# One more quarter-tile of tokens by gathered expert rows, dense expert sums with columns on the partitions, and one-hot gate rows made four at a time with the gates applied on ScalarE

## What is computed

```python
def peer(h, w_query, sub_keys, u_emb, v_emb):
    q = (t @ w_query).reshape(T, PEER_HEADS, 2, PEER_HALF)
    s = jnp.einsum('thpk,pnk->thpn', q, sub_keys)
    s_val, s_idx = lax.top_k(s, PEER_TOPK)                      # 16 of 128, twice a head
    cand = s_val[..., 0, :, None] + s_val[..., 1, None, :]
    best, pos = lax.top_k(cand.reshape(T, PEER_HEADS, 256), PEER_TOPK)
    expert = ...                                                # 128 expert numbers a token
    gate = jax.nn.softmax(best, -1)
    act = jax.nn.gelu(jnp.einsum('td,ted->te', tb, u_emb[eb]), approximate=False) * gb
    return jnp.einsum('te,ted->td', act, v_emb[eb])
x = x + ga2 * peer(modulate(rmsnorm(x, g_ffn), sh2, sc2), ...)
return rmsnorm(x, g_final)
```

## Time and profile before

| | us |
|---|---|
| median of 3 runs | 3695.62 |
| lowest, highest | 3694.08, 3696.91 |
| the profiled execution, its time | 3693.22 |
| its span, first to last instruction | 3691.2 |
| PE busy in the span | 3508.3 |
| DVE busy | 2088.9 |
| POOL busy | 1987.5 |
| ACT busy | 1104.4 |

### The profile page before, as it was taken

The page is one execution under the profiler, slowest core; times in us unless marked ns, Lnnn a source line. Parts: engine busy times, 40 slices in busy tenths (PEclk is TensorE's granted clock), DMA queues, the critical chain, the costliest instruction groups (busy, mean ns, idle before and its releaser), DMA issues.

```text
span 3691.2 us, 46132 instructions
## 1 busy us (share of the span) xinstructions
PE 3508.3 (95%) x17646; PEld 3001.0 (81%) x17646; DVE 2088.9 (57%) x3619; ACT 1104.4 (30%) x1240; POOL 1987.5 (54%) x942
## 2 busy tenths in 40 slices
PE   5799999998889799999999999999999999999996
PEld 2477778874578589999999999999888888888885
DVE  1317561102521365995477777772566776667669
ACT  3221211123322223232344333443232232232222
POOL 0244432211333545677655565556677777777773
PEclk8799999999999899999999999999999999999998
DMA  9545552228632323777666777668898888888883
GB/s 344 208 162 181 186 179 75 79 71 296 249 125 93 124 90 134 250 295 276 250 259 262 292 283 282 258 261 342 319 338 315 311 311 309 317 321 313 305 308 111
DMA packets 291479, 874.83 MB, mean 237 GB/s; under 512 B 17361, under 2 KB 78081, under 8 KB 237216
## 3 DMA queue, kind: packets, MB, share of 16 engines
q1 hardware_dynamic: 226224, 519.08, 40.0%
q0 software_dynamic: 38704, 281.20, 18.7%
q10 hardware_dynamic: 26432, 73.02, 5.2%
HBM read 803.82 MB, written 69.37 MB: 237 GB/s over the span
## 4 chain that ended last, share of the span: by engine, by line
PE 83%; DVE 6%; DMA 5%; ACT 2%; POOL 2%; issue 1%; ACTq 1%; SPq 0%; DVEq 0%
PE bank L1753 76%; PE bank L2032 2%; PE bank L1946 2%; DMA neurons<-tiny 2%; PE bank L1761 2%; DMA ring<-in_w_mod 2%; DMA ring<-in_w_in 1%; PE bank L1925 1%; POOL ring_lo L432 1%; DVE low L1343 1%; DVE acc L1642 1%; ACT w_hi L425 0%; PE bank L2015 0%; DVE b L1531 0%; ACTq L734 0%
## 5 line engine op out<-in xcount | busy, mean ns | idle before, releaser
L692 POOL TENSOR_TENSOR split<-ring,split 128x1024 fp32r<-128x1024 f32 x544 | 1305.6, 2412 | 689.7 <-ACT split L1012 688.8
L1753 PE MATMUL bank<-h_hi,split 128*128 128x384 f32 (+1 forms) x4608 | 1221.0, 342 | 5.2 <-POOL split L692 3.7
L1753 PE MATMUL bank<-split,a_split 128*128 128x512 f32 x4608 | 1052.1, 390 | 17.1 <-DVE acc L1635 8.8
L1012 ACT ACTIVATE split<-ring 128x1024 fp32r<-128x1024 f32 x544 | 577.2, 1062 | 1595.0 <-PE bank L1753 1566.0
L1753 PEld LDWEIGHTS bank<-split,a_split 128*128 128x128 f32 x4608 | 867.4, 188 | 201.7 <-DVE acc L1635 6.2
L1753 PEld LDWEIGHTS bank<-h_hi,split 128*128 128x128 f32 x4608 | 838.0, 188 | 26.3 <-POOL split L692 4.6
L1753 PE MATMUL bank<-h_lo,split 128*128 128x384 f32 (+1 forms) x2304 | 784.0, 340 | 0.0
L432 POOL TENSOR_TENSOR ring_lo<-ring,w_hi 128x2048 fp32r<-128x2048 f32 x47 | 230.4, 4903 | 432.4 <-ACT w_hi L425 427.6
L1753 PEld LDWEIGHTS bank<-h_lo,split 128*128 128x128 f32 x2304 | 433.0, 188 | 9.9
L1635 DVE TENSOR_TENSOR acc<-acc,bank 128x512 f32<-128x512 f32 x360 | 244.4, 682 | 299.8 <-PE bank L1753 281.2
L1753 PE MATMUL bank<-hT_hi,w_hi 128*128 128x512 f32 (+1 forms) x768 | 292.0, 380 | 23.3 <-POOL ring_lo L432 18.5
(11 more groups left out here) (266 smaller groups left out, 3606.2 us busy)
## 6 DMA issues: line engine op xcount, KB each, us to landing
ring<-in_u_emb SPq DMA_DIRECT2D x128, 1024.0 KB
ring<-in_v_emb SPq DMA_DIRECT2D x128, 1024.0 KB
ring<-in_w_mod SPq DMA_DIRECT2D x96, 1024.0 KB
ring<-in_w_in SPq DMA_DIRECT2D x48, 1024.0 KB
neurons<-tiny ACTq DMA_DIRECT2D x128, 192.0 KB
gate_table<-b ACTq DMA_DIRECT2D x6, 4096.0 KB, 14.7
weigh<-neurons SPq DMA_DIRECT2D x32, 768.0 KB
weigh<-gate_table SPq DMA_DIRECT2D x32, 768.0 KB
```

What stands on the lines that cost most here:

```text
L692: nc.gpsimd.tensor_tensor(split[:, r % 2, 1, at].bitcast(F32R), ring[:, r % 4, :, :].rearrange("p k n -> p (k n)")[:, at], split[:, r % 2, ...
L1012: nc.scalar.activation(split[:, q % 2, 0, at].bitcast(F32R), ring[:, q, :, :].rearrange("p k n -> p (k n)")[:, at], ACT.Copy)\
L1753: last = mm(out_, left[a].bitcast(F32R), right[b].bitcast(F32R), start=start and n == 0, stop=stop and n == 2)
```

## The change

It does five things.

1. **Tokens.** The dense tokens become 352 (`TD = 352`, eleven pieces of 32). The 32 tokens 352 to 383 are computed by gathered rows too. They have 128 slots each, and since a gather brings 128 rows, four of a token's slots go into one gather: 32 more gathers in each stage, 160 instead of 128 (`SROWS`). ACT's DMAs spread their row numbers, gates and inputs over the partitions in unit 40 (12 small DMAs). Their dots (n from 128) take both inputs from SBUF (`h2_x` and the rows), and their sums go to `x_acc` in SBUF (both inputs of L1749 in SBUF). The gathers are placed by a formula: one a unit up to gather 34, then 125 in 88 units of the neuron stage (the new ones at units 102 to 124), and 159 in 119 units of the sum stage (the new ones at units 97 to 121).
2. **Neuron units.** The moving operand has 352 columns in place of 384, read as pieces of 32 tokens.
3. **Sum units.** Stationary is now a 128-column piece of `v_emb`'s split, moving is `a_split` with 352 tokens: 4 x 4 x 3 = 48 matmuls of 352 a unit in place of 36 of 512, and four banks of 352 columns a unit are flushed into `acc` [column, token]. At the end PE turns `acc` back, a quarter of the columns at a time (`turn_quarter`), and adds the four parts of the 32 tokens with one matmul.
4. **Gate groups.** 88 in place of 96. DVE makes the first-key rows of four tokens in one instruction, and the second-key rows without gates (`equal`) in another. ACT multiplies by the gate's parts, 8 activations of 128 x 128 a group with the gate as a per-partition scale (`gate_rows`), placed between its two high halves of the unit before. 8 groups lie in 6 units, the table is stored as 2 MB after each 8.
5. **End.** x is loaded as twelve 128 x 512 tiles; the last pass writes and stores each of the twelve alone.

The core of the diff:

```diff
-CHUNK = 64
+XT = 32
+XQ, GT = P // XT, XT
+XROWS = SLOTS // XQ
+SROWS = SLOTS + XROWS
 JD = LT - 1
-TD = JD * P
+TD = JD * P - XT
-CHUNK_UNITS = 12
-GROUPS_AT = (0, 0, 2, 1, 2, 1, 2, 2, 1, 2, 1, 2)
+CHUNK_UNITS = 6
+GROUPS_AT = (0, 1, 2, 1, 2, 2)
...
+def gather_unit(n):
+    return 2 + n if n <= 34 else 36 + (n - 34) * 88 // 125
+def gather_unit_v(m):
+    return 2 + m * 119 // 159
...
+            def gate_rows(grp):
+                act.wait_ge(equal_made, grp + 1)
+                for s in range(4):
+                    tok = slice(4 * grp + s, 4 * grp + s + 1)
+                    for part, gates in enumerate((gate_hi, gate_lo)):
+                        last = nc.scalar.activation(onehot[:, grp % 2, 1 + part, s, :].bitcast(F32R),
+                                                    equal[:, grp % 2, s, :], ACT.Copy, scale=gates[:, tok])
+                last.then_inc(onehot_made, 1)
...
                 for h in range(2):
                     if h < len(groups):
-                        stage_group(*groups[h])
+                        stage_group(2 + groups[h] + 1, 4 * (groups[h] % 8))
                     next_hi(unit, q, h)
+                    if h == 0:
+                        for grp in ahead:
+                            gate_rows(grp)
...
-                nc.vector.tensor_tensor_reduce(out=rows, in0=sparse_bank, in1=rows, scale=1.0, scalar=0.0,
+                tokens = sparse_bank if n < SLOTS else h2_x.rearrange("p (b n) -> p b n", b=4)
+                nc.vector.tensor_tensor_reduce(out=rows, in0=tokens, in1=rows, scale=1.0, scalar=0.0,
...
-                nc.vector.scalar_tensor_tensor(sparse_bank, rows, act_s[:, m:m + 1], sparse_bank, ALU.mult, ALU.add)\
+                nc.vector.scalar_tensor_tensor(sums, rows, act_s[:, m:m + 1], sums, ALU.mult, ALU.add)\
                     .then_inc(rows_used, 1)
...
+                        last = mm3(bank[:, 4 + dt, 0:TD],
+                                   [split[:, k % 2, h, a * NB + dt * P:a * NB + (dt + 1) * P] for h in range(2)],
+                                   [a_split[:, s, h, a, :] for h in range(2)], a == 0, a == GROUP - 1)
...
+            def turn_quarter(q):
+                pe.wait_ge(sum_free, 4 * (NK - 4 + q) + 4)
+                for j in range(JD):
...
+                    for dt in range(4):
+                        last = nc.tensor.transpose(bank[0:width, j, dt * P:(dt + 1) * P],
+                                                   acc[:, 4 * q + dt, j * P:j * P + width], ident)
+                    if width < P:
+                        pe.wait_ge(x_scaled, 1)
+                        last = mm(bank[P - XT:P, j, :], pick_x, x_acc[:, q * NB:(q + 1) * NB], start=True, stop=True,
+                                  tile_position=(0, P - XT))
```

More of the change, by code:

```diff
@@ L1674, in _ @@
                 g = unit // 4
[L1675 removed]
+                last_group = g == GROUPS - 1
+                flush_here = merge if last_group else flush
                 flush_here(unit, 0)
@@ L2070, in _, with tables @@
                     last.then_inc(slotT_full, 1)
+            def tables(unit, chunk, k):
+                first = sum(GROUPS_AT[:k])
+                return [(chunk * 8 + (g + 1), g % 2) for g in range(first, first + GROUPS_AT[k])]
             pe.sem_inc(onehot_used, 2)
-            with pe.Fori(0, CHUNKS) as chunk:
-                group = 0
-                for k in range(CHUNK_UNITS):
-                    groups = [(chunk * 16 + (g + 1), g % 2) for g in range(group, group + GROUPS_AT[k])]
-                    neurons(chunk * CHUNK_UNITS + (PRE + k), k % 4, groups)
-                    group += GROUPS_AT[k]
@@ L2079, in _ @@
-            for k in range(PRE + CHUNKS * CHUNK_UNITS, NK):
+            with pe.Fori(0, CHUNKS // 2) as two:
+                for k in range(2 * CHUNK_UNITS):
+                    neurons(two * (2 * CHUNK_UNITS) + (PRE + k), k % 4,
+                            tables(k, two * 2 + k // CHUNK_UNITS, k % CHUNK_UNITS))
+            for k in range(CHUNK_UNITS):
+                neurons(LAST_CHUNK + k, (LAST_CHUNK + k) % 4, tables(k, CHUNKS - 1, k))
+            for k in range(LAST_CHUNK + CHUNK_UNITS, NK):
```

422 lines of the change are left out of this document (240 added, 182 removed).

## The result

The changed kernel takes 3739.51 us (median of 4 runs, 3734.59 to 3743.03), the kernel before 3694.85 beside it: a ratio of 1.0118, 95% interval 1.0101 to 1.0136. The forecast was 3668 us, faster; the change makes the kernel 1.2% slower, inside the range of 3590 to 3755.

What follows compares the result with a forecast made beforehand. PE's matmuls, 76% of the span, were taken as the bound. Terms of -81.9, -61.4, -6.8, +30, +8, +22, +53, +4 and +5 summed to -28 us, giving a forecast of 3668 us, range 3590 to 3755.

Steps and rivals of the forecast that it cites:

- neuron columns: Neuron units: 128 units x 48 matmuls, each falling from 173.3 to 160.0 ns: -81.9 us on PE.
- gate rows on ACT, hold of bank 6: Gate stretch: ACT's activations, 2.1 us a group, delay its copy of bank 6, which PE awaits: +30 us.
- search, and the units up to 43: While DVE searches, POOL waits for dots before its next gather; PE, arriving earlier, loses time: +8 us.
- added gathers, neuron stage: Units 110 to 124: new dots and POOL shut each other out, POOL needs 9.6 us a unit: +22 us.
- sum units 2 to 96 (with DMA's +4): POOL needs 7.0 and DVE some 6.5 of 7.68 us a unit: no loss; DMA at 366 GB/s: +4 us.
- sum units 97 to 121: Additions in SBUF collide with POOL, which needs 10.1 us a unit against PE's 7.68: +53 us.
- rival A: Gate stretch: activations cost 3.2 us a group, ACT becomes the bound, +115 in place of +30: 3753 us; chance 0.18.
- rival C: Sum stage: DMA keeps up at most 349 GB/s, 8.05 us a unit, +36: 3704 us; chance 0.14.
- The line through three widths: PE matmuls: 13.3 ns plus 0.417 ns a column, from 256, 384 and 512 columns; 160 ns for 352.
- Rival D: Matmuls of 352 columns in eleven pieces of 32 cost the 173 ns of 384: 3832 us; chance 0.05.
- Rival B: Dots and sums of the added rows don't collide with POOL, 22 and 53 us fall away: 3593 us; chance 0.12.
- What would show it: Forecast wrong if sum units before 97 exceed 7.9 us, later ones are under 8.5, or ACT exceeds 95% in gate stretch.

Runs made afterwards that it cites:

- experiment 9: Changed kernel, with POOL issuing each gather of the sum stage between the two rests of the next unit: 3698.66 us, ratio 1.0006 to the kernel before.
- experiment 7: Changed kernel, with sum-stage gathers issued between the next unit's two rests and a unit's second row added behind the third flush: 3685.54 us.
- experiment 4: Changed kernel, with product and rest taking their second input from PSUM instead of SBUF (sums not the reference's): 3676.25 us, ratio 0.9949 to the kernel before.
- experiment 5: Changed kernel, with the neuron stage's moving operand read as 352 adjacent columns, not eleven pieces of 32 (neurons not the reference's): 3714.39 us.
- experiment 6: Changed kernel, with the sums of the 32 added rows kept in PSUM instead of x_acc in SBUF: 3697.18 us, ratio 1.0002 to the kernel before.
- experiment 3: Changed kernel, loading only half of the rows of v_emb for the dense sums (sums not the reference's): 3736.77 us, ratio 1.0119 to the kernel before.

## Why the prediction was wrong, step by step

The terms of the forecast's sum, and what the two profiled executions show for each, by the table of stages and the plain units (us):

| step | forecast | traces |
|---|---|---|
| neuron columns | -81.9 | 128 x (7.89 - 8.32) = -55 |
| sum units | -61.4 | 128 x (7.63 - 8.16) = -68 |
| gate groups on PE | -6.8 | -8 x 0.90 = -7.2 |
| gate rows on ACT, hold of bank 6 | +30 | 11 x 3.77 = +41.5 |
| first groups of the stretch | 0 | +5 |
| search, and the units up to 43 | +8 | +9 |
| added gathers, neuron stage | +22 | +4 |
| sum units 2 to 96 (with DMA's +4) | +4 | +57 |
| sum units 97 to 121 | +53 | +54.5 |
| last six units, end | +5 | 0 |
| sum | -28 | +41 |

That the measured time lies in the stated range is luck: the range's upper end, 3755, was rival A's, with ACT as the bound of the gate stretch, and ACT is busy 70% of it. The dearest case below it was rival C's 3704, and most of the time was lost where the forecast put nothing.

*The step that failed* is the sentence "In units 2 to 96 the additions go to PSUM and POOL needs 7.0 of 7.68 us, DVE some 6.5 (...): no loss, beside short ones". It put at nothing what measured 57 us. It counted what each engine has to do in a unit and took both as independent. It left out three things that the code and the rows of before held. The product and the rest have two SBUF inputs, and the earlier trace rows showed one waiting for POOL; the forecast priced that in units 97 to 121, and here it used 1.2 us a unit for both, where the trace has (5.16 + 3.18) / 4 = 2.1. The four banks of a unit are now filled in 1.91 us each and not in 2.72, so a flush may be 5.7 us late and not 8.2. And the row buffers come round in 17.2 us and not 24.5, so POOL waits for DVE while DVE waits for POOL. The first two alone don't explain the loss: with the gathers half a unit later (experiments 9 and 7) the same instructions in the same banks lose 0.3 and 0.13 us a unit in place of 0.61. That the shut-outs in the product and the rest are what cost is shown by experiment 4, which takes only these away: its units take 7.82 us. How much the phase owes to the buffers and how much to rests that run back to back is open.

*Neuron columns.* The line through three widths held for adjacent columns: 159 ns in the sum stage, where it gave 160. In the neuron stage the operand lies in eleven pieces of 32, and a matmul takes 164.4. Rival D named the pieces and gave them all or nothing; they cost 4.4 of the 13.3 ns, 27 us, by experiment 5.

*Gate rows.* The mechanism, the unit and the wait are as forecast, 2.06 us against 1.9; the 0.8 us that the forecast gave to a chunk's other units is not there. The size was off twice. An activation of 128 columns with a scale from SBUF starts 0.29 us behind the one before it, not 0.25; the row taken was for two instructions of 512 columns. The Trainium skill (ScalarE: Activation LUTs, on what an ACTIVATE costs) has a price by columns, with one for each per-partition operand; an estimate from its figures is 0.39 us for one such activation and 0.29 from one to the next, and the trace agrees with 387 ns and 0.29. And the hold costs 1.7 us more through the clock, which the forecast left out everywhere. One step of its sum does not come out as written: 0.71 less 0.42 is 0.29 and not 0.40; its step from 0.57 to 0.25 takes 0.32 for the same 384 columns, and by that the row gives 0.39. The upper bound of 3.2 us a group and rival A rest on that row; of rival A's +115 us only 11 x 3 = 33 were worked out. Rival A had put the point where ACT becomes the bound at 2.5 us a group; at 2.35 it isn't.

*Sum units 97 to 121.* 9.83 us a unit against the 10.1 forecast, and experiment 6 shows the cause to be the one named: in PSUM the same sums take 2.35 us in place of 3.6 to 4.2, and the units 8.31. Rival B fell here. It was right for the dots of the neuron stage, in part: they last 2.7 to 3.7 us there, DVE and POOL shut each other out, but the 18 units lose only 4 us, since DVE had little else to do and the gathers' buffers were free.

*DMA.* The forecast's +4 was nothing, and its rival C is refuted by experiments 3 and 4. A share of 1.00 at 369 GB/s goes with PE busy 99% of the time. Where transfers did matter, once ACT's work had been moved, was in the stores, which no term named.

*What would show it* was right to name units before 97 over 7.9 us, and wrong to read them as rival C.

## What to carry to other kernels

Where two engines shut each other out and also hand each other buffers, a sum of what each has to do in a unit is no bound: ask how long each buffer takes to come round, and what the engine that waits for it has queued behind. When a stage gets shorter, every tolerance in it does too, in banks and in buffers, and so each order that was free before has to be walked through again with the new times. A short wait of the bounding engine can cost nearly twice its length once its clock falls (here 3.8 us for 2.06), and removing a hold uncovers what it had covered, here a store of 2 MB.

## What the runs showed of the hardware that I had not expected

- PE's granted clock is at half (1.2 GHz, not 2.4) for 3.4 or 6.8 us at or behind all eleven waits of 2.06 to 2.09 us in the gate stretch, and behind five of the eight waits of 2.19 to 2.21 us in sum units 2 to 96: those five units take 11.7 us, the other three 10.1. Behind the six waits of 1.5 to 1.8 us in the same units it doesn't fall. In the kernel before it is at half for 10 us between 1435 and 3674 us, in the kernel after for 113 between 1435 and 3713. What decides when it falls was not tried.
- 352 moving columns in eleven pieces of 32 take 164.4 ns, adjacent ones 159 to 160.
- Issuing POOL's gathers half a unit later, with the second row behind the third flush, moved the mean of a DVE instruction from 5.16 to 1.83 us, with the same operands.
- A gather's issue on POOL takes 0.96 us alone and 1.6 to 2.2 in mean, by buffer, in the units where DVE takes dots or row sums with both inputs in SBUF; with the row sums in PSUM it is 1.1 to 1.2 in sum units 97 to 121.
